# One ring of u and v row pairs split into a ring of u rows and a ring of v rows

## The reference

```python
def one_block(xb):                                 # 128 tokens
    q = (xb @ w_query).reshape(L, PEER_HEADS, 2, PEER_QUERY_DIM // 2)
    s = jnp.einsum('lhpd,hpkd->lhpk', q, sub_keys)
    ...                                            # top 16 of each side, top 16 of the 256 sums
    expert = jnp.take_along_axis(cidx, pos, axis=-1)      # 8 heads x 16 = 128 experts per token
    gate = jax.nn.softmax(best, axis=-1)
    u = expert_u[expert]
    v = expert_v[expert]
    h = jax.nn.gelu(jnp.einsum('ld,lhkd->lhk', xb, u), approximate=False)
    return jnp.einsum('lhk,lhkd->ld', (h * gate).astype(xb.dtype), v)
```

## Time and profile before

| | us |
|---|---|
| three timed runs | 3285.55, 3289.55, 3303.25 |
| median | 3289.55 |
| the profiled execution's own time | 3286.67 |
| its span, first to last instruction | 3284.9 |

### The profile page before, as it was taken

How to read it: one execution, slowest core, us unless ns; L and a number is a source line. 1 busy time by engine, 2 the same in 40 slices (tenths; PEclk the granted TensorE clock), 3 DMA queues, 4 the chain that set the end, 5 groups by cost and what they waited for, 6 DMA issues and landing times.

```text
span 3284.9 us, 37869 instructions
## 1 busy us (share of the span) xinstructions
PE 2458.7 (75%) x11896; PEld 1369.7 (42%) x11896; DVE 2231.3 (68%) x5593; ACT 1140.9 (35%) x3499; POOL 1187.5 (36%) x1028
## 2 busy tenths in 40 slices
PE   8886778867788577967779677886788867776554
PEld 6673335523355233643346333553345523351111
DVE  3368755986568765788558875597656876579444
ACT  3213532244233533335333353234423353332222
POOL 0023442334432443334432345233443244323443
PEclk9998899988899898998988888997889979886777
DMA  8069999999999999999999999999999999989997
GB/s 330 7 260 387 417 415 404 389 404 387 408 385 412 397 412 404 382 413 397 419 398 385 393 416 407 401 396 404 382 407 390 405 377 412 401 355 352 420 420 321
DMA packets 194040, 1254.26 MB, mean 382 GB/s; under 512 B 22312, under 2 KB 22440, under 8 KB 59696
## 3 DMA queue, kind: packets, MB, share of 16 engines
q0 software_dynamic: 147456, 1073.81, 80.2%
q1 hardware_dynamic: 44208, 172.67, 13.3%
q10 hardware_dynamic: 2176, 5.36, 0.4%
HBM read 1247.56 MB, written 4.19 MB: 381 GB/s over the span
## 4 chain that ended last, share of the span: by engine, by line
DMA 32%; PE 32%; DVE 19%; ACT 9%; issue 5%; POOL 2%; DVEq 0%; POOLq 0%; SPq 0%; ACTq 0%
DMA ring<-in_uv,expert_used 23%; PE expert_sum L792 13%; DMA chunk<-in_weights 9%; DVE ring L1456 8%; PE bank L514 7%; PE bank L503 4%; POOL ring L452 2%; ACT diag L1036 2%; PE bank L521 1%; PE bank L617 1%; ACT arena L896 1%; PE bank L526 1%; DVE arena L1404 1%; DVE arena L1407 1%; ACT h_raw L1029 1%
## 5 line engine op out<-in xcount | busy, mean ns | idle before, releaser
L452 POOL DMA_INDIRECT ring<-in_uv,expert_used x1024 | 1187.3, 1159 | 2067.2 <-PE expert_sum L792 1597.6
L792 PE MATMUL expert_sum<-ring,diag 128*64 128x512 f32 x4096 | 1207.1, 718 | 642.0 <-ACT diag L1036 641.5
L1456 DVE CUSTOM_DVE_ANT_0 ring<-ring,x_pair 128x1024 f32<-128x1024 f32 x1024 | 1231.4, 1222 | 594.3 <-DMA ring<-in_uv,expert_used 589.5
L792 PEld LDWEIGHTS expert_sum<-ring,diag 128*64 128x64 f32 x4096 | 313.8, 156 | 1281.4 <-issue 1267.0
L1029 ACT ACTIVATE h_raw<-h_raw 128x2 f32<-128x2 f32 x512 | 104.1, 203 | 1544.0 <-DVE h_raw L1456 1543.3
L1036 ACT ACTIVATE diag<-const,h_raw 128x64 f32<-128x64 f32 x1024 | 292.8, 333 | 0.0
L1032 ACT ACTIVATE h_raw<-h_raw,gate_used 128x1 f32<-128x1 f32 x1024 | 245.6, 286 | 16.8
L514 PE MATMUL bank<-o_cat,chunk 128*128 128x128 f32 x1376 | 184.0, 292 | 42.5 <-DMA chunk<-in_weights 42.4
L514 PEld LDWEIGHTS bank<-o_cat,chunk 128*128 128x128 f32 x1376 | 170.1, 203 | 83.3 <-DMA chunk<-in_weights 60.6
L514 PEld LDWEIGHTS bank<-oT,chunk 128*128 128x128 f32 x1344 | 152.8, 192 | 22.7 <-issue 22.7
L514 PE MATMUL bank<-oT,chunk 128*128 128x128 f32 x1344 | 158.7, 277 | 0.0
(11 more groups left out here) (239 smaller groups left out, 2534.3 us busy)
## 6 DMA issues: line engine op xcount, KB each, us to landing
chunk<-in_weights SPq DMA_DIRECT2D x266, 512.0 KB, 11.6
ring<-in_uv,expert_used POOLq DMA_INDIRECT x1024, 11.9
ring<-in_weights SPq DMA_DIRECT2D x15, 1024.0 KB, 20.1
o_cat<-in_xT SPq DMA_DIRECT2D x8, 512.0 KB, 15.2
kept<-in_weights SPq DMA_DIRECT2D x4, 1024.0 KB, 14.5
chunk<-in_weights SPq DMA_DIRECT2D x4, 1024.0 KB, 17.1
x<-in_x SPq DMA_DIRECT2D x8, 512.0 KB, 15.6
out<-oT ACTq DMA_DIRECT2D x8, 512.0 KB, 9.2
```

Source lines behind the costliest of these rows:

```text
L452: pool.indirect_dma_start(out=ring[:, (j % RING) * 2 * D:(j % RING + 1) * 2 * D], out_offset=None, in_=io["uv"], in_offset=bass.IndirectOf ...
L792: mm = pe.matmul(expert_sum[i][c * SPAN:(c + 1) * SPAN, :], diag[:, (j % DIAGS) * SPAN:(j % DIAGS + 1) * SPAN], ring3[:, j % RING, D + i * ...
L1456: dve.tensor_tensor_reduce(u, u, x_pair[:, (j % 2) * D:(j % 2 + 1) * D], 1.0, 0.0, ALU.mult, ALU.add, h_raw[:, j:j + 1]).then_inc(dotted.s ...
```

## The change

The row table is read as 32768 rows of 4 KB (`uv_rows`), where row 2e is expert e's u and row 2e + 1 its v. Each slot gets two indirect DMAs, u first and then v, each of 128 rows of 4 KB. The 64 KB per partition of the ring are divided into U_RING = 6 slots for u and V_RING = 10 slots for v, numbered on over the blocks. A u slot is free after `dotted`, a v slot after `added`. VectorE waits for u alone; TensorE waits for v. The picks end with two more operations on 128x32 (2 x number, and 2 x number + 1) and with a second `by_pair` of four casts. The order of the gathers on GpSimd is u0, v0, u1, v1, and so on, with a wait before each.

```diff
-RING = 8
+U_RING, V_RING = 6, 10
...
-        ring = sb("ring", RING * 2 * D)
+        ring = sb("ring", (U_RING + V_RING) * D)
...
-        expert_used = sb("expert_used", SLOTS, U32)
+        u_used = sb("u_used", SLOTS, U32)
+        v_used = sb("v_used", SLOTS, U32)
...
-        gathered = [signal(f"gathered{i}", 16 * len(range(i, SLOTS, RING))) for i in range(RING)]
-        dotted = signal("dotted", SLOTS)
+        u_in = [sem(f"u_in{i}") for i in range(U_RING)]
+        v_in = [sem(f"v_in{i}") for i in range(V_RING)]
+        dotted = signal("dotted", SLOTS, before=U_RING)
...
-        added = signal("added", SLOTS, before=RING)
+        added = signal("added", SLOTS, before=V_RING)
...
-        DVE_STEPS, ACT_STEPS, LN_STEPS = 94, 6, 7
+        DVE_STEPS, ACT_STEPS, LN_STEPS = 98, 6, 7
...
+        def u_rows(n, j):
+            r = (n * SLOTS + j) % U_RING
+            return ring[:, r * D:(r + 1) * D]
+        def v_rows_of(n, j):
+            r = U_RING + (n * SLOTS + j) % V_RING
+            return ring[:, r * D:(r + 1) * D]
+        def u_there(n, j):
+            return u_in[(n * SLOTS + j) % U_RING], 16 * ((n * SLOTS + j) // U_RING + 1)
+        def v_there(n, j):
+            return v_in[(n * SLOTS + j) % V_RING], 16 * ((n * SLOTS + j) // V_RING + 1)
...
+        uv_rows = io["uv"].rearrange("e (s c) -> (e s) c", s=2)
...
-            def gathers(n, first=0):
-                for j in range(first, SLOTS):
+            def gathers(n):
+                for j in range(SLOTS):
                     if j % PART == 0:
                         pool.wait_ge(*staged.at(n, 1 + j // PART))
                         alone(pool)
-                    pool.wait_ge(*added.at(n, ring_free(j)))
-                    gather(j)
...
+                    if n == 0 and j < U_RING:
+                        early_weights_done(j)
+                    else:
+                        pool.wait_ge(*dotted.at(n, j - U_RING + 1))
+                    alone(pool)
+                    pool.indirect_dma_start(
+                        out=u_rows(n, j), out_offset=None, in_=uv_rows,
+                        in_offset=bass.IndirectOffsetOnAxis(ap=u_used[:, j:j + 1], axis=0),
+                    ).then_inc(u_there(n, j)[0], 16)
+                    if n == 0 and j < V_RING:
+                        early_weights_done(U_RING + j)
+                    else:
+                        pool.wait_ge(*added.at(n, j - V_RING + 1))
+                    alone(pool)
+                    pool.indirect_dma_start(
+                        out=v_rows_of(n, j), out_offset=None, in_=uv_rows,
+                        in_offset=bass.IndirectOffsetOnAxis(ap=v_used[:, j:j + 1], axis=0),
+                    ).then_inc(v_there(n, j)[0], 16)
...
-                        pe.wait_ge(*gathered[j % RING].at(n, arrived(j)))
+                        pe.wait_ge(*v_there(n, j))
...
-                                           ring3[:, j % RING, D + i * 512:D + (i + 1) * 512],
+                                           v_rows_of(n, j)[:, i * 512:(i + 1) * 512],
...
-                    by_pair(expert_used, pos_hi, i * PART, (i + 1) * PART).then_inc(staged.sem, 1)
+                    ts(pos_lo[:, two], pos_hi[:, two], 2.0, 1.0, ALU.mult, ALU.add)
+                    then(n, ts(pos_hi[:, two], pos_hi[:, two], 2.0, None, ALU.mult))
+                    by_pair(u_used, pos_hi, i * PART, (i + 1) * PART)
+                    by_pair(v_used, pos_lo, i * PART, (i + 1) * PART).then_inc(staged.sem, 1)
...
-                        dve.wait_ge(*gathered[j % RING].at(n, arrived(j)))
-                        u = ring3[:, j % RING, 0:D]
+                        dve.wait_ge(*u_there(n, j))
+                        u = u_rows(n, j)
```

More of the change, by code:

```diff
@@ L57 @@
 STREAMED = [c for c in range(CHUNKS) if c not in KEPT]
-EARLY = 2 + RING * 2 * D // (KT * W)
+EARLY = 2 + (U_RING + V_RING) * D // (KT * W)
 TWO_PI = (6.28125, 2029.0 / 2 ** 20, 2 * math.pi - 6.28125 - 2029.0 / 2 ** 20)
@@ L344, in build @@
         vrows = v_rows[:, :].rearrange("p (s c) -> p s c", s=2)
-        ring3 = ring[:, :].rearrange("p (r c) -> p r c", r=RING)
+        def u_rows(n, j):
[8 more added lines that the diff above has]
+            return v_in[(n * SLOTS + j) % V_RING], 16 * ((n * SLOTS + j) // V_RING + 1)
         A_ROT, A_T = 16, 10
@@ L427, in _, with early_weights_done @@
             sp.wait_ge(*stored.at(NB, 0))
[L429 to L436, removed]
+        uv_rows = io["uv"].rearrange("e (s c) -> (e s) c", s=2)
         @block.gpsimd
         def _(pool):
-            def gathers(n, first=0):
-                for j in range(first, SLOTS):
+            def early_weights_done(r):
+                place = 2 + r * D // (KT * W)
+                pool.wait_ge(*chunk_used.at(0, 1 + max(c for s, c in enumerate(STREAMED) if s % EARLY == place)))
+            def gathers(n):
+                for j in range(SLOTS):
                     if j % PART == 0:
@@ L445, in gathers @@
                         alone(pool)
-                    pool.wait_ge(*added.at(n, ring_free(j)))
-                    gather(j)
[L450 to L463, removed]
+                    if n == 0 and j < U_RING:
[16 more added lines that the diff above has]
+                    ).then_inc(v_there(n, j)[0], 16)
+            for n in range(NB):
                 gathers(n)
@@ L529, in _ @@
             pe.sem_inc(chunk_used.sem, 1)
-            pe.sem_inc(added.sem, RING)
+            pe.sem_inc(added.sem, V_RING)
             def ln_row(banks, row, done):
@@ L1098, in _ @@
             dve.memset(conv_in[:, :], 0.0).then_inc(conv_tail.sem, 1)
-            for unused in (rows_staged, sums_read, out_ready):
+            for unused in (rows_staged, sums_read, out_ready, dotted):
                 dve.sem_inc(unused.sem, unused.before)
```

## The result

The kernel after takes 3470.11 us (median of 4 runs, 3461.14 to 3481.1), the kernel before 3287.55 us (4 runs): a ratio of 1.0567, 95% interval 1.0533 to 1.0600. The change costs some 183 us. The forecast was 3405 us, its range 3280 to 3500.

The account below looks back on a forecast made before the run. The prediction took the DMA engines as the limit before the change. GpSimd issue +115, small packets +21, earlier release -25 and index work +5 made +116 us on the 3289.55 us median: 3405 us, range 3280 to 3500.

Parts of the forecast that it names:

- The deciding term: GpSimd's gather issue: two per slot take 2.78 us against 2.56 in dense stretches, +88 us; +115 with the last block.
- The slots thought free: In the other 529 slots two issues fit even with delays; only smaller packets cost there, +21 us.
- The last block: GpSimd paces 96 slots between 3010 and 3250 us at 2.78 us in place of 2.50: +27 us.
- The first rival: DMA engines stay the limit, gathers and products fall into step at 2.5 us: 3316 us; chance 0.20.
- The small packets: Gather queue: 4 KB packets cost 0 to +82 us if DMA limits throughout, middle +41; +21 us entered the sum.
- The lead: u slots free once VectorE has dotted, so u rows are requested earlier: -25 us, between 0 and -49.
- The ceiling itself: While gathers run, some 68 us of DMA time are idle, of which 49 us at most could be won.
- one of the prediction's signs: DMA shares fall to 0.90 to 0.93 in the dense stretches; staying at 1.00 would favour the DMA-limit rival.
- The other signs: 262144 packets of 4 KB, GpSimd gaps mostly 0.30 us, VectorE's row waits longer, GpSimd busy near 2048 x 1.15 us.
- The index work: Added operations and casts per pick, 38 us on VectorE, mostly hidden by its row waits: +5 us, +38 uncovered.
- The strict lock: No part of a gather runs beside a product: 3.10 us per slot, some 3580 us; chance 0.08, near cases included.

Follow-up runs that it names:

- the sum: VectorE's product replaced by a plain sum over the same 1024 columns: 3327.4 us in the kernel after, 3272.99 us in the kernel before.
- the split kernel: The kernel after, with separate u and v gathers of 4 KB rows: 3470.11 us; the name is also used for its variants.
- the joint one: The kernel before, with one gather of 8 KB rows per slot, here with VectorE's product replaced by a plain sum: 3272.99 us (ratio 0.9969).
- the short product: VectorE's product cut to the first 256 of 1024 columns: 3258.94 us in the kernel after, 3198.11 us in the kernel before.
- eight slots each: The kernel after with eight u and eight v slots in place of six and ten, u still free when dotted: 3445.15 us (1.0459).
- the split kernel without the lead: The kernel after with eight u and eight v slots, both free only when TensorE has added: 3650.45 us (1.1102).
- half the bytes: The kernel after gathering rows of 2 KB in place of 4 KB, with the same 2048 gathers: 3565.82 us (1.0862).

## Why the prediction came out right, and 65 us low

*The deciding term.* GpSimd's pace was put at 2.78 us per slot for the stretches that the DMA engines had paced. Mid-block it is 2.79 us; there the slots take (2.79 - 2.56) x 57 = 13 us more in the block shown, 92 us over seven if they are like it, against 88 forecast. Taking the holds away (the sum) gives 143 us back in the split kernel and 10 in the joint one, so 133 of the 187 us between the two go with the product and not with the sum: the holds. The step and its mechanism were right.

*The slots thought free.* The prediction let the other stretches of a block pass two issues "even with delays" and gave them 21 us in all for packets. They are where most of the missing time lies. A block of the seven grew by 24 us, and 13 of that are in the dense stretches; the other 11, 80 us over seven, fell outside. A mean of 3.0 us per slot hides bursts: GpSimd stops for indices (118.8 us) and for u slots (253.8 us), and then refills at 2.8 us per slot where it refilled at 1.24 to 1.5. The waits are in the trace; that they are the cause in these very stretches was argued from them and not tried apart.

*The last block.* +27 us was forecast, +15 came. Products and gathers are in step there at 2.56 us, and the DMA engines are at their limit for 4 KB packets, 409 GB/s as in the short product (columns as in the earlier trace rows):

```profile
3300.00:3350.00 50.00, 29.13 (x80) 7.22 (x80) 24.50 (x39) 10.73 (x46) 38.02 (x40) 0.70 1.03 409
```

At that rate the 1.05 MB of a slot take 2.56 us too, so here the two limits meet. The first rival, in which the DMA engines stay the limit and the issues fall into step, was right for this block and wrong for the seven others.

*The small packets.* With both kernels at the limit of the DMA engines, 409 against 420 GB/s, the split kernel is 61 us slower, second issue and lead included. That lies between the ends 0 and +82; the packets' price alone was not measured.

*The lead.* -25 us was forecast, from a ceiling of 49 us of idle DMA time. Measured, the release of u by VectorE is worth 180 us in the split kernel, 205 with eight slots each. The term was mis-sized because it was weighed in the kernel before, where DMA bytes limit, and not in the kernel after, where the queue of GpSimd does: there a wait of GpSimd costs time.

*The ceiling itself.* "49 us at most could be won" was wrong as well: the short product runs the joint kernel in 3198 us with the same bytes, 85 us less. A DMA share of 0.99 was read as saturation. But the first seven blocks, at 0.98 to 0.99, moved 396 to 403 GB/s (two of them in the earlier trace rows), while a stretch at the limit moves 420. The GB/s is the row to read. The same 4 KB packets are booked with more time where the engines are pressed less: 80.9% of 3471 us, 2808 us, in the kernel after, and 82.9% of 3257 us, 2700 us, with the short product. What fills it is not shown. It also undid one of the prediction's signs: the share in the dense stretches was to fall to 0.90 to 0.93, and a share of 1.00 was to speak for the first rival. It stayed at 0.97 to 1.00, while the rate, 409 to 420 GB/s before, fell to 360 to 382. The other signs came: 262144 rows of 4 KB, gaps of 0.30 us, longer waits of VectorE for its rows, a mean gather of 1.10 us.

*The index work.* +5 was forecast, with +38 if nothing hid it. Removing it gave 32 us, near the uncovered end: VectorE's waits for rows were no cover. A likely reason, not tried apart, is that once GpSimd sets the pace, what delays the indices or a u slot's release delays GpSimd.

*The strict lock.* It was not borne out: a v gather that starts while 0.2 us of a product are left loses 0.07 us, and a u gather that overlaps a product for 0.7 us loses nothing.

In sum, against +116: the split kernel without the lead is 367 us slower, the lead gives 180 back. Of the 187 left 133 are holds and 54 the rest, in which packets and index work are. That the total came within 65 us is in part luck. Without its lead the forecast had the change at +141 us, 226 too little, and it had the lead at 25, 155 too little; the two errors have opposite signs and mostly cancel.

## What to carry to other kernels

The cost of a software-issued gather is per instruction, not per byte: before cutting transfers finer, multiply the count by the issue time and compare it with the time per slot in the densest stretch and with the speed of refills after a wait, not with the mean over the kernel. Size each term of a change in the kernel as it will be: the lead that was put at 25 us from the idle DMA time of the kernel before was worth 180 us in the kernel after. And read the GB/s beside the DMA share; here the share was between 0.97 and 1.01 for anything from 360 to 420 GB/s.

## What the runs showed of the hardware

- A gather of 128 rows takes GpSimd 0.94 to 0.95 us undisturbed and 0.30 us until the next, with rows of 8 KB, 4 KB, 2 KB and 4 bytes alike; the means beside products are 1.10 us with 8 KB and 1.11 us with 4 bytes.
- VectorE's product, with two SBUF inputs, holds a gather's issue; a sum over the same 1024 columns with one input, 1215 ns long, does not: 963 ns in place of 1099. The Trainium skill (SBUF — State Buffer, "Who interferes with whom") says of both that they behave so: two SBUF inputs contend with a GpSimd instruction that reads SBUF, `tensor_reduce` never contends. Its sentence that the second comer is blocked entirely is written for VectorE's modes that use both ports. Taken for this product, it does not fit the last block's rows, where gathers and products overlap by up to 0.7 us at no cost.
- A gather that begins inside a product ends 0.80 to 0.82 us behind it (48 of 48 in the last block of the kernel before); one that begins 0.15 to 0.2 us ahead of a product is not held. So which gathers are held is a matter of phase: with half the bytes the last block's slots took 3.0 us, with all of them 2.56 us.
- At their limit the 16 DMA engines moved 409 GB/s with rows of 4 KB and 420 GB/s with rows of 8 KB.
